# A chunked scan beside a matmul stream: the turns move to unit 16 of their own group, where the former group's sum of squares now stands too

## What is computed

```python
def step(state, inp):
    xc, dtc, bc, cc = inp
    cum = jnp.cumsum(dtc * a, axis=1)
    decay = jnp.exp(jnp.where(causal, cum[:, :, None] - cum[:, None], -jnp.inf))
    w = jnp.einsum('bign,bjgn->bijg', cc, bc)[..., None] * decay * dtc[:, None]
    y = jnp.einsum('bijgh,bjghp->bighp', w, xc)
    y = y + jnp.einsum('bign,bghpn->bighp', cc, state) * jnp.exp(cum)[..., None]
...
y = y.reshape(bsz, seq, SSM_D_INNER) * jax.nn.silu(z.astype(f32))
yg = y.reshape(bsz, seq, g, SSM_D_INNER // g)
yg = yg * lax.rsqrt(jnp.mean(yg * yg, axis=-1, keepdims=True) + EPS)
```

## Time and profile before

| | |
|---|---|
| median of 3 runs | 2573.61 us |
| the profiled execution | 2574.58 us, of which 2572.9 us are the span of the trace |
| PE busy | 2566.3 us of the span |
| DVE, ACT, POOL busy | 1790.5, 1415.8, 220.2 us |

### The profile page before, as it was taken

How to read it: one execution, slowest core, us unless ns; L and a number is a source line. 1 busy time by engine, 2 the same in 40 slices (tenths; PEclk the granted TensorE clock), 3 DMA queues, 4 the chain that set the end, 5 groups by cost and what they waited for, 6 DMA issues and landing times.

```text
span 2572.9 us, 46087 instructions
## 1 busy us (share of the span) xinstructions
PE 2566.3 (100%) x15225; PEld 2253.1 (88%) x15225; DVE 1790.5 (70%) x2592; ACT 1415.8 (55%) x2182; POOL 220.2 (9%) x197
## 2 busy tenths in 40 slices
PE   9999999999999999999999999999999999999999
PEld 8888888888888888888888888888888888888888
DVE  8778777875677777775555686767777777775444
ACT  6676767754455555554444465675555555554333
POOL 0211122112100000000111000102200000000000
PEclk9999999999999999999999999999999999999999
DMA  6655555656555555556666675334555556556665
GB/s 213 230 198 193 196 198 197 201 179 189 179 196 191 190 189 187 190 191 185 189 190 192 193 234 200 116 98 140 186 190 189 188 186 194 188 188 187 189 191 169
DMA packets 139483, 481.59 MB, mean 187 GB/s; under 512 B 17329, under 2 KB 19441, under 8 KB 138384
## 3 DMA queue, kind: packets, MB, share of 16 engines
q1 hardware_dynamic: 136448, 467.20, 56.9%
q0 software_dynamic: 2368, 12.68, 1.4%
q10 hardware_dynamic: 592, 0.71, 0.1%
HBM read 478.28 MB, written 2.16 MB: 187 GB/s over the span
## 4 chain that ended last, share of the span: by engine, by line
PE 89%; DVE 5%; ACT 3%; issue 2%; DMA 1%; POOL 0%; ACTq 0%; DVEq 0%; SPq 0%; POOLq 0%
PE ps L838 48%; PE ps L837 25%; PE pq L838 5%; PE po L838 3%; PE pq L837 3%; DVE w_lo L1258 2%; PE po L837 1%; ACT w_hi L441 1%; DMA raw<-w_ssm_in 1%; PE po L1141 1%; DVE cv L1366 1%; ACT wcum L536 1%; PE pq L1127 0%; PE ps L897 0%; PE pq L855 0%
## 5 line engine op out<-in xcount | busy, mean ns | idle before, releaser
L1258 DVE TENSOR_TENSOR w_lo<-raw,w_hi 128x1024 fp32r<-128x1024 f32 (+1 forms) x896 | 1093.7, 1223 | 613.3 <-ACT w_hi L441 612.1
L441 ACT ACTIVATE w_hi<-raw 128x1024 fp32r<-128x1024 f32 (+1 forms) x896 | 933.3, 1043 | 797.6 <-PE ps L838 695.7
L838 PE MATMUL ps<-xn,w_hi 128*128 128x512 f32 x3904 | 1358.6, 391 | 0.0
L837 PE MATMUL ps<-xn,w_lo 128*128 128x256 f32 x3904 | 1098.5, 281 | 0.3 <-DVE gpad L1267 0.2
L838 PEld LDWEIGHTS ps<-xn,w_hi 128*128 128x128 f32 x3904 | 730.4, 187 | 159.0
L837 PEld LDWEIGHTS ps<-xn,w_lo 128*128 128x128 f32 x3904 | 737.8, 189 | 4.9 <-DVE w_lo L1258 1.9
L838 PE MATMUL ps<-hid,w_hi 128*128 128x512 f32 x1408 | 488.2, 391 | 0.0
L837 PE MATMUL ps<-hid,w_lo 128*128 128x256 f32 x1408 | 394.2, 280 | 0.0
L838 PEld LDWEIGHTS ps<-hid,w_hi 128*128 128x128 f32 x1408 | 263.3, 187 | 57.7
L837 PEld LDWEIGHTS ps<-hid,w_lo 128*128 128x128 f32 x1408 | 266.1, 189 | 0.0
L838 PE MATMUL pq<-xn,w_hi 128*128 128x512 f32 x528 | 184.3, 391 | 0.0
(11 more groups left out here) (299 smaller groups left out, 2444.8 us busy)
## 6 DMA issues: line engine op xcount, KB each, us to landing
raw<-w_gu SPq DMA_DIRECT2D x352, 512.0 KB, 3.9
raw<-w_ssm_in SPq DMA_DIRECT2D x158, 512.0 KB, 3.8
raw<-w_down SPq DMA_DIRECT2D x128, 448.0 KB, 3.4
raw<-w_nsa_in SPq DMA_DIRECT2D x82, 512.0 KB, 4.2
raw<-w_ssm_out SPq DMA_DIRECT2D x64, 512.0 KB, 3.7
raw<-w_down SPq DMA_DIRECT2D x64, 512.0 KB, 3.6
raw<-w_nsa_out SPq DMA_DIRECT2D x32, 512.0 KB, 4.3
wcum<-cum_scratch POOLq DMA_DIRECT2D x8, 1024.0 KB, 7.6
```

What stands on the lines that cost most here:

```text
L441: act.activation(w_hi[:, slot, 0:n * P], raw[:, slot, 0:n * P], ACT.Copy).then_inc(unit_rounded, 1)
L837: pe.matmul(acc[:, n:2 * n], w_lo[:, slot, cols], x[:, kb, 0:n], start=(kb == 0), stop=False, skip_group_check=True)
L838: mm = pe.matmul(acc[:, 0:2 * n], w_hi[:, slot, cols], x[:, kb, 0:2 * n], start=False, stop=(kb == n_blocks - 1), skip_group_check=True)
L1258: TT(w_lo[:, slot, 0:n * P], raw[:, slot, 0:n * P], w_hi[:, slot, 0:n * P].bitcast(F32), ALU.subtract).then_inc(unit_split, 1)
```

## The change

The turn of group g moves from unit 0 of body g+1 to unit 16 of body g, and the sum of squares of group g-1 moves from unit 14 to unit 16 of that body, right ahead of the turn. It gets another PSUM bank (`ps[5]`; so a wait for the finished tile 6 ahead of it, and one for the square root at unit 2 of the next body). On ACT the exponentials move from 3, 4, 5 to 0, 1, 2, `scan_std` from 14 to 17, `scan_round` from 16 to 19. On DVE `scan_xdt` moves to 17 of the own body, `scan_w` from 5 to 3, `scan_norm` from 15 to 18 and `scan_rest` to 0 of the next body but one of its group. POOL masks right behind the sum of squares, and multiplies x by D afterwards. In body 1 the exponentials stay at 3, 4, 5.

```diff
-            SCAN_ACT = ((1, scan_sbt), (3, scan_ecum), (3, lambda g: scan_decay(g, 0)), (4, lambda g: scan_decay(g, 1)),
-                        (11, scan_square), (14, scan_std), (16, scan_round))
+            SCAN_ACT = ((0, 1, scan_ecum), (0, 1, lambda g: scan_decay(g, 0)), (1, 1, lambda g: scan_decay(g, 1)),
+                        (2, 1, lambda g: scan_decay(g, 2)), (11, 1, scan_square), (17, 0, scan_sbt), (17, 1, scan_std),
+                        (19, 1, scan_round))
...
                 pe.wait_ge(conv_act, 6 * g + 6)
                 pe.wait_ge(tk_ready, 1)
                 pe.wait_ge(xdt_ready, g)
-                pe.wait_ge(gstd_ready, g)
...
             def scan_sumsq(g):
+                total = ps[4] if is_body(g, GROUPS - 1) else ps[5]
                 pe.wait_ge(sq_summed, g + 1)
...
+                if not is_body(g, GROUPS - 1):
+                    pe.wait_ge(tile_out, ph["ssm"].tile0 + 7 + (g + 1) * ph["ssm"].per_body)
+                pe.matmul(total[:, 0:T], ones[:], xdt[:, 0, 0:T], start=True, stop=True).then_inc(gss_done, 1)
...
-            SCAN_PE = ((0, scan_turn), (9, scan_y), (14, scan_sumsq))
+            SCAN_PE = ((9, 1, scan_y), (16, 1, scan_sumsq), (16, 0, scan_turn))
...
+                    if scan and v == 2:
+                        pe.wait_ge(gstd_ready, g - 1)
...
-            SCAN_DVE = ((1, scan_xdt), (5, scan_w), (10, scan_yz), (15, scan_norm), (17, scan_rest))
+            SCAN_DVE = ((0, 2, scan_rest), (3, 1, scan_w), (10, 1, scan_yz), (17, 0, scan_xdt), (18, 1, scan_norm))
...
-                if not is_body(g, 0):
+                if is_body(g, 0):
+                    pool.wait_ge(cum_landed, 32)
+                else:
                     sum_squares(g - 1)
-                pool.wait_ge(conv_act, g * 6 + 6)
-                pool.wait_ge(y_ready, g)
-                pool.wait_ge(cum_landed, g * 32 + 32)
-                pool.tensor_tensor(yz[:], xf[:], cst[:, bass.ds(g * XT_G + CONST["ssm_d"], XT_G)].unsqueeze(2).broadcast_to([P, XT_G, T]),
-                                   ALU.mult).then_inc(xd_ready, 1)
...
                 mask(0)
                 mask(1).then_inc(cum_masked, 1)
+                pool.wait_ge(conv_act, g * 6 + 6)
+                pool.wait_ge(y_ready, g)
+                pool.tensor_tensor(yz[:], xf[:], cst[:, bass.ds(g * XT_G + CONST["ssm_d"], XT_G)].unsqueeze(2).broadcast_to([P, XT_G, T]),
+                                   ALU.mult).then_inc(xd_ready, 1)
```

More of the change, by code:

```diff
@@ L65 @@
 PLAIN_TILES = 1
+FIRST_LATER = 3
 UNITS_OF = {16: [8, 8], 32: [8, 8, 8, 8], 44: [8, 7, 7, 8, 7, 7]}
@@ L543, in scan_std @@
             def scan_std(g):
+                total = ps[4] if is_body(g, GROUPS - 1) else ps[5]
                 act.wait_ge(gss_done, g + 1)
-                act.activation(grs[:], ps[4][:, 0:T], ACT.Sqrt, scale=1.0 / (XT_G * P), bias=eps[:, 0:1]).then_inc(gstd_ready, 1)
+                act.activation(grs[:], total[:, 0:T], ACT.Sqrt, scale=1.0 / (XT_G * P), bias=eps[:, 0:1]).then_inc(gstd_ready, 1)
             def scan_round(g):
@@ L557, in ssm_body @@
                         conv_first(p, g, k - 1, k - 1)
-                    if v % 2 and v == DECAY_ENDS and scan:
-                        scan_decay(g - 1, 2)
                     if v % 2:
@@ L566, in ssm_body @@
                         z_silu(g, k - 7)
[L567 to L571, removed]
+                    if not scan:
                         dt_part(v)
+                    for at, back, stage in SCAN_ACT:
+                        if at + (FIRST_LATER if at < 3 and is_body(g, 1) else 0) == v and (scan or not back):
+                            stage(g - back)
                 z_silu(g, 3)
-            DECAY_ENDS = 5
-            SCAN_ACT = ((1, scan_sbt), (3, scan_ecum), (3, lambda g: scan_decay(g, 0)), (4, lambda g: scan_decay(g, 1)),
-                        (11, scan_square), (14, scan_std), (16, scan_round))
+            SCAN_ACT = ((0, 1, scan_ecum), (0, 1, lambda g: scan_decay(g, 0)), (1, 1, lambda g: scan_decay(g, 1)),
+                        (2, 1, lambda g: scan_decay(g, 2)), (11, 1, scan_square), (17, 0, scan_sbt), (17, 1, scan_std),
+                        (19, 1, scan_round))
             p = ph["ssm"]
@@ L583, in last_scan_step @@
             def last_scan_step(v):
-                for at, stage in ((1, scan_sbt), (2, scan_ecum), (2, lambda g: scan_decay(g, 0)), (2, lambda g: scan_decay(g, 1)),
+                for at, stage in ((2, scan_ecum), (2, lambda g: scan_decay(g, 0)), (2, lambda g: scan_decay(g, 1)),
                                   (2, lambda g: scan_decay(g, 2)), (6, scan_square), (8, scan_std), (9, scan_round)):
@@ L969, in scan_sumsq @@
             def scan_sumsq(g):
+                total = ps[4] if is_body(g, GROUPS - 1) else ps[5]
                 pe.wait_ge(sq_summed, g + 1)
-                pe.matmul(ps[4][:, 0:T], ones[:], xdt[:, 0, 0:T], start=True, stop=True).then_inc(gss_done, 1)
+                if not is_body(g, GROUPS - 1):
+                    pe.wait_ge(tile_out, ph["ssm"].tile0 + 7 + (g + 1) * ph["ssm"].per_body)
+                pe.matmul(total[:, 0:T], ones[:], xdt[:, 0, 0:T], start=True, stop=True).then_inc(gss_done, 1)
             p = ph["ssm"]
-            SCAN_PE = ((0, scan_turn), (9, scan_y), (14, scan_sumsq))
+            SCAN_PE = ((9, 1, scan_y), (16, 1, scan_sumsq), (16, 0, scan_turn))
             def ssm_body(g, scan=True):
                 for v in range(0 if scan else 4, p.body):
+                    if scan and v == 2:
+                        pe.wait_ge(gstd_ready, g - 1)
                     gemm_unit(p, g, v, xn)
[L979 to L983, removed]
+                    for at, back, stage in SCAN_PE:
+                        if at == v and (scan or not back):
+                            stage(g - back)
+                    if not scan and v == 15:
                         turn_dt()
@@ L989, in _ @@
             for v in range(p.body):
-                if v == 6:
-                    pe.wait_ge(y_ready, GROUPS - 1)
+                if v == 0:
+                    pe.wait_ge(y_ready, GROUPS - 2)
+                if v == 3:
+                    pe.wait_ge(gstd_ready, GROUPS - 1)
                 if v == 12:
@@ L994, in _ @@
                 gemm_unit(p, 0, v, y_ssm)
-                for at, stage in ((0, scan_turn), (6, scan_y), (8, scan_sumsq)):
+                for at, stage in ((6, scan_y), (8, scan_sumsq)):
                     if at == v:
@@ L1425, in ssm_body @@
                         conv_pad(p, g, k)
[L1426 to L1429, removed]
+                    for at, back, stage in SCAN_DVE:
+                        if at + (FIRST_LATER - 1 if stage is scan_w and is_body(g, 1) else 0) == v and (not back or scan and (back == 1 or not is_body(g, 1))):
+                            stage(g - back)
                     if taps:
@@ L1446, in last_scan_step @@
             def last_scan_step(v):
-                for at, stage in ((1, scan_xdt), (6, scan_yz), (8, scan_norm), (9, scan_rest)):
+                if v == 0:
+                    scan_rest(GROUPS - 2)
+                for at, stage in ((6, scan_yz), (8, scan_norm), (9, scan_rest)):
                     if at == v:
```

1 line of the change is left out of this document (added).

## The result

The changed kernel takes **2585.81 us** (median of 5 runs, 2585.51 to 2587.34) where the kernel before takes 2573.69 beside it (2572.65 to 2574.49): a ratio of **1.0047, 95% interval 1.0036 to 1.0058**, 12.1 us slower. The forecast was 2576.1, its range ended at 2580.2. The execution that was profiled is the slowest of the five, 1.5 us over their median.

A forecast was written before the change was run, and what follows sets the result against it. PE was taken to set the time, so only its stops and work besides the units count. Terms -1.8 - 0.7 + 1.7 + 3.3 = +2.5 us gave a median of 2576.1 us, range 2571.5 to 2580.2.

The forecast's parts named there:

- the burst: Instructions added up around a body's edge, bodies 2 to 7: split 5 goes before `cex`, split 8 is 0.55 us late.
- the second rival: POOL's `cex` takes the port before split 5: 1.4 us in 6 bodies, 8.4; 2581.2 us; chance 0.13.
- Sums of squares, -1.8: At the sum of squares, all 1.8 us of waiting for POOL go, since the product moves two units later.
- Side by side, -0.7: Turn directly behind the sum of squares: the slow first pair's 0.19 us per body saved or paid; taken as -0.7 us.
- First turn, +1.7: Turn behind unit 16 of body 0: PE waits 2.0 us for `tk`, 0.3 saved at `scan_y` of body 1; net +1.7.
- Unit 8, +3.3: Bodies 2 to 7: a new wait of 0.55 us for split 8 in each, +3.3 us, bounds 0 to 6.6.
- The last group, 0: In `ssm_out` turn and work move earlier by about as much; priced at nothing, or some tenths once without the splits' lead.
- no change: Whole kernel: +2.5 us, 2576.1, within the 0.2% (5.1 us) that a measurement can't tell from no change; chance 0.50.

The follow-up runs named there:

- experiment 2: The changed kernel with one needless memset of 128x8 elements on POOL between `yz` and `cex`; 2578.34 us, ratio 1.0018.
- Experiment 8: The kernel before, with only the sum of squares one unit later (15), and root, norm, rounding and rest one unit later too; 2572.35 us, ratio 0.9994.
- experiment 1: The changed kernel with POOL's product of `cex` ahead of that of x with D, from the second group on; 2578.90 us, ratio 1.0016.
- Experiment 6: The changed kernel with `cex` ahead of x·D on POOL and `scan_w` back behind unit 5 instead of 3; 2574.70 us, ratio 1.0002.
- experiment 4: The changed kernel with the first group's turn, `scan_sbt` and `scan_xdt` back in body 1, behind units 0 and 1; 2587.86 us, ratio 1.0051.

## Why the prediction was wrong

**The step that failed** is in the burst: "Split 5 is ready at 21.3, is held until 21.45 and done at 22.55: 1.1 ahead of PE. Then POOL's `cex`". The times were right. Counted from the turn's start at 382.21, the rounding of unit 5 ends at 21.35 (21.3 in the prediction) and `yz` at 21.41 (21.45). Who follows was wrong: `cex` started at 21.38, and the split ended at 24.87, where the second rival has 24.95. Its price, 1.4 us in 6 bodies or 8.4, measured 6.7 + 2.3 = 9.0. I gave it a chance of 0.13, because at 324.91 a waiting split had gone ahead of POOL's next instruction. That row was no model of this place. There the split had been waiting for 1.4 us when `yz` ended; here the rounding and `yz` end together, and POOL's next instruction started 0.01 us ahead. The rival's own condition, "when the rounding of unit 5 ends after `yz`", was not even needed: the rounding ended 0.06 before it. With a margin of 0.15 in a chain for which I myself allowed an error of 0.5, the two orders should have been held about equally likely.

The trace agrees with what the Trainium skill, "SBUF — State Buffer", section "SBUF: two separate sides", says of an exclusive lock that the first one keeps for its whole instruction: 3.48 for the split behind `cex`, and 3.47 for `cex` behind the split in experiment 2.

The other terms:
- **Sums of squares, -1.8:** right; their waits for POOL are gone. The 1.8 are idle time of the weight loads ahead of the product; by PE's own starts the waits had cost 1.6. Experiment 8 shows that one unit would have done, not two.
- **Side by side, -0.7:** mis-sized, it was nothing. Sum and turn together take 1.88 (381.78 to 383.66). In experiment 8, where they stand apart, PE's rows at the sum are these:

```profile
306.46 0.59 PE L971 MATMUL po<-xdt,ones 128*128 128x256 f32 x2
306.70 0.47 PE L837 MATMUL pq<-xn,w_lo 128*128 128x256 f32 x1
307.01 0.40 PE L838 MATMUL pq<-xn,w_hi 128*128 128x512 f32 x1
```

  The sum takes 0.24, the pair behind it loses 0.19 (0.31 to its second product, where 0.12 is normal), and the turn takes 1.45 elsewhere: 1.88 again. Beside the turn the 0.19 is paid there, the upper bound of the loss that I had named.
- **First turn, +1.7:** right. PE stood 2.0 longer than its even 0.23 (66.87 to 69.06), and of the 0.6 at `scan_y` of body 1 0.4 came back: its start is 0.49 behind the last product there (107.13 to 107.62), against 0.87 before. That makes 1.6. The table has 2.1 at this place because the pairs of body 1 were slower too, by 0.6 (below). How much comes back there differs between executions: in experiments 1, 2 and 6, with the same early turn, the gap at `scan_y` is 0.80 to 1.19 again, and in experiment 8, whose instructions up to there are those of the kernel before, it is 0.32, as in the other bodies. Experiment 4 shows that the table loads named in that step are real (2.56 us), and that without the early turn they cost as much as the early turn does.
- **Unit 8, +3.3:** the size was right as long as the split goes first: 2.8 in experiment 1, and 0.54 to 0.58 where the bodies run evenly. In the changed kernel it was 2.3, since PE itself was 1.2 late by then. Experiment 6 shows that `scan_w` at 3 was its cause.
- **The last group, 0:** nothing is added there in the table above; right.
- **Not in the sum at all:** PE's even stream itself became slower. These rows of the changed kernel, PE in body 3 and in body 5, are each the first and last of four product pairs:

```profile
254.69 0.40 PE L837 MATMUL pq<-xn,w_hi 128*128 128x512 f32 x1
...
256.10 0.40 PE L837 MATMUL pq<-xn,w_hi 128*128 128x512 f32 x1
...
378.09 0.39 PE L837 MATMUL pq<-xn,w_hi 128*128 128x512 f32 x1
...
379.48 0.39 PE L837 MATMUL pq<-xn,w_hi 128*128 128x512 f32 x1
```

Four pairs in 1.41, or in 1.39: 0.353 or 0.347 for one (in a slow stretch one pair of three takes 0.347 and two take 0.356). Over all pairs from 60 to 560 us without a stop the excess over the even pace is 0.7 us before and 2.9 after, and of this 0.1 and 0.7 lie ahead of `scan_y` of body 1.

So the 12.8 us of span are: sums of squares -1.6, side by side 0, first turn +1.6, stops at units 5 and 8 +9.0, the first pairs behind them +1.3, the slower pace +2.3. That is 12.6, good to some 0.2; and 0.2 are there already at 60 us, ahead of all that was moved (a product that starts at 60.07 before starts at 60.27 after). What sets a pair's pace stays open. The waits alone do not: experiment 4 has the same six waits at unit 5 (5.7 us in the view of the waits), and an excess of 0.8 only. But the pace nearly always changes at a break in the stream: of the 29 longer stretches between two breaks (a stop, a turn, a `scan_y`) in the changed kernel, 26 keep one pace nearly throughout, 10 of them the slow one. Since it differs between executions with the same stops, a part of the 2.3 may belong to the profiled execution alone; that isn't shown.

The forecast of "no change" fell with that one step: without it (experiment 2) the same kernel stands at 1.0018, within the bound, 4.3 us above the kernel before where 2.5 were forecast.

## What to carry to other kernels

Where two engines share a resource that one of them takes for a whole instruction, and their requests come within a few tenths of a us, price both orders and give them like chances; a row in which one engine had long been waiting doesn't say who wins a close race. Such an order can be set cheaply, by swapping two instructions of the blocking engine or by moving one away from the place, and a wait of half a us at the bottleneck needed one unit of room here, not a new schedule. When a step is moved earlier to make room, list what its first instance waits for in the start-up, because that instance has no steady state behind it.

## What the hardware showed unexpectedly

- **A fill of 0.11 us bought nearly 8 us.** A split whose input came 0.06 us before POOL's `yz` ended was behind POOL's next instruction by 0.01 to 0.02 us in six bodies of six; with the fill between, it was 0.03 ahead.
- **Two paces of the same product.** A pair of matmuls takes 0.347 us or, in the mean of three, 0.353, and the stream mostly holds one of the two from one break to the next. The cause is open.
- **The granted clock after a stop.** In experiment 4 PE was idle for 2.20 us, and the clock in the stretch behind it was 0.68: 1.00 (2.4 GHz) until 108.1, then 0.50 (1.2 GHz) from 108.2 to 111.5, single products of `scan_y` going from 0.27 to 0.42 us, and 0.99 in the stretch behind that. In the changed kernel PE was idle for 1.80 at 66.9, and the table by stretch shows 1.00 behind it:

```profile
62.00:66.90 4.90, 4.90 (x32) 4.13 (x30) 4.06 (x6) 4.87 (x7) 0.00 (x0) 1.00 0.61 207
66.90:69.10 2.20, 0.40 (x4) 0.11 (x3) 1.93 (x2) 2.20 (x6) 0.00 (x0) 1.00 0.62 212
69.10:72.00 2.90, 2.90 (x20) 2.70 (x21) 2.07 (x3) 1.23 (x2) 1.51 (x2) 1.00 0.75 196
```

PE was busy throughout ahead of both stops. They differ in length and in what followed (`scan_y` there, a turn and the even stream here); whether either matters, these rows don't show.
